# A streaming-encoder block on one core: the third head's recurrence begins one slot later

## What is computed

```python
D_MODEL = 1024; SEQ = 512; HG_HEADS = 4          # one batch, one layer, f32
for l in range(DEPTH):
    x = x + 0.5 * swiglu(rmsnorm(x, ffn1_norm[l]), ffn1_w_gu[l], ffn1_w_down[l])
    x = x + token_mixing(rmsnorm(x, mix_norm[l]), w_in[l], ...)
    x = x + cross_attention(rmsnorm(x, xa_norm[l]), rmsnorm(mem, mem_norm[l]), ...)
    x = x + 0.5 * swiglu(rmsnorm(x, ffn2_norm[l]), ffn2_w_gu[l], ffn2_w_down[l])

def token_mixing(h, w_in, lb, hg_norm, conv_w, conv_norm, w_out):
    p = h @ w_in
    q, fz, i, g, gb, gc, u = split(p)            # 512 columns each
    f = lb + (1 - lb) * sigmoid(fz);  k = 1 - f
    # four heads of 128 columns: S_t = diag(f_t) S_{t-1} + k_t v_t^T,  o_t = S_t^T q_t
    o_hg = hgrn2_chunkwise(silu(q), log(f), k, i)
    o_hg = rmsnorm(o_hg, hg_norm) * silu(g)
    o_cv = rmsnorm(gb * causal_dwconv(gc * u, conv_w), conv_norm)
    return concatenate([o_hg, o_cv]) @ w_out
```

## Time and profile before

| | before |
|---|---|
| median of 3 runs | 1094.02 us (1093.92 to 1094.51) |
| the profiled execution's own time | 1094.52 us |
| its span, first to last instruction | 1092.7 us |
| granted TensorE clock | 0.999 of full speed |
| PE busy | 1080.1 us, 99% of the span |
| DVE busy | 638.7 us, 58% |
| ACT busy | 527.1 us, 48% |
| POOL busy | 442.9 us, 41% |

### The profile page before, as it was taken

The page is one execution under the profiler, slowest core; times in us unless marked ns, Lnnn a source line. Parts: engine busy times, 40 slices in busy tenths (PEclk is TensorE's granted clock), DMA queues, the critical chain, the costliest instruction groups (busy, mean ns, idle before and its releaser), DMA issues.

```text
span 1092.7 us, 17701 instructions
## 1 busy us (share of the span) xinstructions
PE 1080.1 (99%) x6520; PEld 957.9 (88%) x6520; DVE 638.7 (58%) x944; ACT 527.1 (48%) x739; POOL 442.9 (41%) x546
## 2 busy tenths in 40 slices
PE   9999999999999999999999999999999999999997
PEld 7889999988888888788789888888899999988886
DVE  7887777582223668988477134465977777531002
ACT  6445555542323656564467343354555555633231
POOL 0010000486665444456458874173000000586550
PEclk9999999999999999999999999999999999999999
DMA  7277775332322222122323442122677665333212
GB/s 246 78 206 200 200 202 173 117 114 98 116 96 100 74 84 71 58 97 78 121 73 132 159 152 78 40 86 76 176 203 191 184 184 171 117 117 115 97 58 78
DMA packets 49459, 136.91 MB, mean 125 GB/s; under 512 B 4736, under 2 KB 11008, under 8 KB 49280
## 3 DMA queue, kind: packets, MB, share of 16 engines
q1 hardware_dynamic: 43888, 118.90, 31.1%
q0 software_dynamic: 4320, 15.73, 8.5%
q10 hardware_dynamic: 1200, 1.57, 0.4%
HBM read 134.09 MB, written 2.10 MB: 125 GB/s over the span
## 4 chain that ended last, share of the span: by engine, by line
PE 52%; POOL 25%; issue 21%; DVE 1%; POOLq 0%; DMA 0%; ACT 0%; DVEq 0%; SPq 0%; ACTq 0%
POOL wl L531 25%; PE bank L1642 8%; PE bank L1644 8%; PE bank L1643 8%; PE bank L1757 4%; PE bank L1756 4%; PE bank L1755 4%; PE score L1757 3%; PE score L1756 3%; PE score L1755 3%; PE bank L1653 2%; PE o_bank L1757 1%; PE o_bank L1756 1%; PE o_bank L1755 1%; PE bank L1711 1%
## 5 line engine op out<-in xcount | busy, mean ns | idle before, releaser
L531 POOL TENSOR_TENSOR wl<-raw,wh 128x256 fp32r<-128x256 f32 x512 | 416.6, 847 | 306.4 <-ACT wh L565 263.7
L565 ACT ACTIVATE wh<-raw 128x1024 fp32r<-128x1024 f32 x120 | 125.8, 1053 | 126.0 <-PE bank L1644 119.4
L1642 PE MATMUL bank<-xh,wh 128*128 128x512 f32 x392 | 157.7, 402 | 0.6 <-DVE V L1521 0.6
L545 POOL DMA_DIRECT2D raw<-w_all x30 | 26.1, 869 | 318.0 <-DMA raw<-w_all 318.0
L1644 PE MATMUL bank<-xh,wl 128*128 128x512 f32 x392 | 153.2, 391 | 0.0
L1643 PE MATMUL bank<-xl,wh 128*128 128x512 f32 x392 | 153.1, 390 | 0.0
L1642 PE MATMUL bank<-zr,wh 128*128 128x512 f32 (+1 forms) x374 | 141.0, 377 | 0.0
L1644 PE MATMUL bank<-zr,wl 128*128 128x512 f32 (+1 forms) x374 | 140.8, 377 | 0.0
L1643 PE MATMUL bank<-zr,wh 128*128 128x512 f32 (+1 forms) x374 | 140.8, 377 | 0.0
L1020 DVE SCALAR_TENSOR_TENSOR x<-bank,x 128x512 f32<-128x512 f32 (+1 forms) x31 | 21.3, 686 | 160.4 <-PE bank L1644 160.1
L578 ACT ACTIVATE wh<-raw 128x1024 fp32r<-128x1024 f32 x50 | 52.9, 1058 | 86.6 <-PE bank L1644 53.8
(11 more groups left out here) (331 smaller groups left out, 2687.4 us busy)
## 6 DMA issues: line engine op xcount, KB each, us to landing
raw<-w_all SPq DMA_DIRECT2D x200, 512.0 KB, 3.3
raw<-w_all POOLq DMA_DIRECT2D x30, 512.0 KB, 5.2
zf<-w_all SPq DMA_DIRECT2D x30, 256.0 KB, 4.4
x<-x_t SPq DMA_DIRECT2D x8, 256.0 KB, 6.0
out_t<-x SPq DMA_DIRECT2D x8, 256.0 KB, 2.4
raw<-w_all SPq DMA_DIRECT2D x6, 256.0 KB, 6.1
memf<-mem_t ACTq DMA_DIRECT2D x1, 1024.0 KB, 4.7
raw<-w_all ACTq DMA_DIRECT2D x2, 256.0 KB, 4.1
```

The source lines that it names most:

```text
L531: ins = nc.gpsimd.tensor_tensor(wl[:, slot, two], raw[:, slot, two], wh[:, slot, two].bitcast(f32), SUB)
L545: pool.dma_start(raw[:, 2 * p + 1, :], w_all[u, :, :], accum_op=ADD).then_inc(up_added[p], 16)
L565: nc.scalar.activation(wh[:, slot, :], raw[:, slot, :], ACT.Copy).then_inc(hi_ready, 1)
L1642: nc.tensor.matmul(out_, a[0], b_[0], start=first, stop=False)
```

## The change

Head 2's steps all move one slot down: A from slot 12 to 13, L0 from 13 to 14, L1 from 14 to 15, L2 from 15 to 16, K from 16 to 17, Q from 17 to 18, S from 18 to 19, O from 19 to 20, N from 20 to 21, the norm on DVE from 21 to 22. Heads 0, 1 and 3 and all units keep their places.

```diff
-HEAD_START = [1, 7, 12, 17]
+HEAD_START = [1, 7, 13, 17]
```

## The result

| | before | with the change |
|---|---|---|
| median, 22 runs each on the same chips | 1094.32 us (1093.72 to 1095.42) | 1096.24 us (1095.15 to 1097.14) |
| the profiled execution's own time | 1094.52 us | 1097.03 us |
| its span | 1092.7 us | 1095.2 us |

The ratio is 1.0017, with a 95% interval of 1.0011 to 1.0023: a loss of 1.9 us, small but real. The forecast was 1094.3 us in a range up to 1096.1; the measured median lies just above that. The kernel before came to 1094.32 over these runs, 0.3 above the median of three runs that the forecast started from, so what the change added was forecast as +0.3 us and measured as +1.9.

What follows compares the result with a forecast made beforehand. PE's own queue was taken as the bound, busy 99% of the span, so only PE's waits count. −1.93 removed, +1.8 at L0(3) and +0.4 at K(3) gave +0.3 on 1094.02: 1094.3 us, range 1092.4 to 1096.1.

Steps and rivals of the forecast that it cites:

- Bare lengths: PE's step times in the mixer without waits, such as 7.05 us for an O step with a unit.
- what is removed: PE's stall in slot 14 ahead of head 2's first scores goes: −1.93 us.
- L0(2), slot 15: Head 2's first two factors ready at 453.8 and 454.5, before PE wants them: cost 0, cover 0.5 to 0.7 us.
- two factors take 1.36: DVE makes the two factors of L0(2), behind ACT's first exp at 453.1, in 1.36 us.
- L0(3), slot 19: PE waits behind S(2) for head 3's second factor, ready 484.8, wanted 483.15: price +1.8 us.
- the 14.70: DVE's time before the change from the silu of q3 to the end of head 3's two first factors, in us.
- The low end: L0(3)'s price without the at most 1.3 us of slow pieces from POOL's conversions: 0.5 us left.
- so the factors end at 484.8: End of head 3's first factors on DVE: 469.05 + 15.16 + 0.6, giving PE a stall of 1.7, with semaphore 1.8 us.
- K(3), slot 21: DVE's levels 4 and 5 ready at 498.9 and 499.6, PE there at 498.8 and 499.3: +0.4 us, between 0 and 0.8.
- The sum: −1.93 + 1.8 + 0.4 = +0.3 us over the kernel before, for a median of 1094.3 us.
- The clean gain: Rival: head 3's scan and factors are in time, giving 1092.1 to 1092.6 us; chance 0.16.
- The contention rival: POOL's twelve conversions hinder DVE from 466 to 485 by 4.3 us: stall 4.8, total 1097.3 us; chance 0.11.

Runs made afterwards that it cites:

- the exps first: Changed kernel with ACT's weight conversion of slot 14 put behind the two exps of L0(2) instead of ahead of them: 1096.84 us, ratio 1.0021.
- a quiet POOL: Low weight parts of slots 20 to 23 made for four columns only, products incomplete: 1093.65 us on the changed kernel, 1094.31 us on the kernel before.
- the filler in slot 19: Changed kernel with eight unread matmuls of ones on PE ahead of head 3's first scores: 1095.77 us, ratio 1.0013.
- the filled one: Kernel before with seven unread matmuls on PE ahead of the first score of L1(2) in slot 14: 1094.41 us, ratio 1.0001.

## Why the prediction was wrong, point by point

- **Bare lengths and what is removed (−1.93): right.** Every stretch without a wait came out as forecast within a few hundredths (O(1) with unit 15 in 7.05, slots 16 to 18 in 20.23 instead of 20.21), and the wait of slot 14 went whole.
- **L0(2), slot 15 (cost 0): wrong, 0.70 in the profiled execution.** The order of events on ACT was right, but the exps ran from 452.8, forecast 452.5, while PE was 0.13 earlier than forecast, which took most of the cover of 0.5; DVE idled 2.88 us, forecast 3. Then the step "two factors take 1.36" failed. They took 1.92, since POOL's conversion begins when ACT's conversion ends, which stands directly ahead of those exps: the meeting is built into the order (1.91 or 1.92 in all five profiled executions that have it, 1.29 with the exps first). How much of it PE feels hangs on the earlier meeting at 434 us: 0.70 where DVE lost it, 0.10 to 0.13 where POOL did. The Trainium skill's page "ScalarE: Activation LUTs", section "What ACT_TABLE_LOAD costs", with its drain of 1.38 us, is not borne out by the trace: from the load's start to that of the exp are 452.79 − 451.50 = 1.29.
- **L0(3), slot 19 (+1.8): right in place, engine and kind, 0.4 low.** Waits of 1.88 and 0.3. The chain began at 469.67 instead of 469.05 and lasted 16.09 (16.0 in the prediction's way of counting) instead of 15.76. What it is made of was judged wrongly: the 14.70 held 2.0 us of meetings with POOL and not "at most 1.3". The row of 1.21 at line 1422 was counted as that operation's length, when it is one of 0.67 that met a conversion. The low end, +0.5 with no meeting at all, came out (0.43 with a quiet POOL), in part by luck: more was saved on the meetings, and more was spent on waiting for the logarithm, 1.06 instead of 0.6.
- **A term that was missing: the clock.** The step "so the factors end at 484.8, stall 1.7, price 1.8" took a wait's price to be its length. In the profiled execution the wait cost 1.6 more. Over all runs it is about 0.5 of the median: runs of the changed kernel without it have a median of 1095.7, inside the range; with it 1096.9.
- **K(3), slot 21 (+0.4): nothing in the profiled execution.** PE came there at 501.42 instead of 498.8, for the reasons above, and DVE's factors, whose chain took 13.4 us (13.46 forecast), were no longer late; slots 20 and 21 took their 15.2 us. With the filler in slot 19, where PE is there at 499.82, they took 15.52: without the slow clock the term is 0.3, close to the forecast.
- **The sum.** +0.3 forecast; with +1.6 (clock), +0.7 (slot 15), +0.4 (slot 19) and −0.4 (K(3)) it is +2.6, as the profiled execution has it. The median moved 1.9: about 0.5 of that is the clock, and the rest, 1.4, is +0.3 with slots 15 and 19 as they were. So even without the clock the loss was several times the forecast one, and in this account the larger part of the difference is slot 15, the place priced at nothing. Where POOL lost the meeting at 434 us the same difference sits elsewhere: slot 15 loses 0.13, but the wait of the kernel before is smaller too and only 1.49 is removed (457.14 − 447.66 = 9.48 in the filled one, less 7.99).
- **The rivals.** The clean gain was not to be had: with POOL quiet the two medians differ by 0.66, not 1.9. The contention rival named a mechanism that is there (1.77 us on DVE's chain by experiment), but at 4.3 us it was priced too high, and it was not new: the order before met POOL for as long. New was that PE waited for the end of that chain. The Trainium skill's page "SBUF — State Buffer", section "Who interferes with whom", calls the shared port pair an exclusive lock, from which the prediction took up to 0.95 us a meeting; here the four rows that a quiet POOL shortened most lost 0.45 to 0.55 each, and most of the twelve conversions met nothing on the chain.

What stays open: which executions get the slow clock, and whether it is always this wait that brings it. Of 94 runs of the kernel before that were taken beside the experiments, four took 1097.2 to 1097.6 us with a mean clock of 0.996 or 0.997, and one run of the changed kernel with the quiet POOL took 1097.0 with 0.996; none of them was profiled. Nor is it shown what decides the meeting at 434 us, or how much of the spread between runs it makes.

## What to carry to other kernels

Before a step is moved to end a wait, sum what the slower engine has to do between the two steps that are drawn together; here DVE had two pauses left, 0.70 and 0.59 us, in a chain of sixteen, so the wait moved along, and only spacing both heads (6, 6 and 5 slots) and putting three places in order took it away. For every operation of that sum look for a shorter row of the same kind and shape elsewhere in the trace, and look whether POOL runs beside it: where another is 0.5 us shorter, the row at hand may hold a meeting, and the new order may add or remove one. The same line is not enough: all four rows of line 1422 in the kernel before last 1.21 to 1.23 us, each beside POOL, and only the shortest rows of the same shape at lines 1415 and 1410, 0.68 and 0.67 us, give it away. A cover shorter than one such meeting is no cover. And a wait of PE of about 2 us may cost twice that, so one long wait may be dearer than several short ones with the same total; the latter was not tested.

## What the runs showed of the hardware

- The granted clock fell to 0.50 behind waits of 1.76, 2.18, 2.42 and 2.73 us of an otherwise full PE and stayed at 1.00 behind waits of 1.52, 1.98, 2.15 and 2.44 us in others. The length of the wait alone doesn't decide it. Nor does one execution speak for a kernel: a mean clock of 0.996 or less had 7 of 22 runs with the wait of 1.76, 4 of 8 with 2.44, 1 of 11 with 2.15, 2 of 9 with 2.42, 7 of 8 with 2.73, and 2 of 94 of the kernel before. Each fall lasted some 3 us and cost about 1.5 (1.6 in slot 19, 1.5 in slot 14 by medians). With eight or eleven products that nobody reads put into the wait no run had it; seven of them where the wait was 1.5 brought nothing.
- DVE beside POOL's 128x256 conversions: a two-input product of 512 columns took 1.13 or 1.22 us instead of 0.67, a difference of 256 columns 0.95 instead of 0.41, a scan 1.78 instead of 1.23. In these rows it is about the same half us whatever the operation's own length. Where a DVE instruction and a conversion started within 0.04 us of each other, either one took the loss: DVE 1.03 and POOL 3.89 us for its four, or 0.47 and 4.46. So these two engines do not meet at semaphores alone.
